# Recurrent stage of a decoder step: normalisation moved to mid-turn, a convolution ahead of the output, the store on another queue

## What is computed

```python
def rglru_block(h, conv_buf, h0, w_in, conv_w, conv_b, w_a, b_a, w_x, b_x, lam, w_out):
    gate_in, xb = jnp.split(h @ w_in, 2, axis=-1)
    gate = jax.nn.gelu(gate_in)
    xcat = jnp.concatenate([conv_buf.astype(xb.dtype), xb], axis=1)
    xc = conv_b + sum(xcat[:, j:j + T] * conv_w[j] for j in range(CONV_W))
    r = jax.nn.sigmoid(einsum('btnc,ncd->btnd', xcb, w_a) + b_a)      # xcb: xc in 8 blocks of 128
    i = jax.nn.sigmoid(einsum('btnc,ncd->btnd', xcb, w_x) + b_x)
    log_a = -RG_C * r * jax.nn.softplus(-lam)
    a = jnp.exp(log_a)
    u = jnp.sqrt(-jnp.expm1(2.0 * log_a)) * (i * xc)
    ...                                   # h_t = a_t * h_(t-1) + u_t along the tokens
    y = hs.swapaxes(0, 1).astype(h.dtype) * gate
    return y @ w_out, hT.astype(h.dtype), new_buf
```

## Time and profile before

| | |
|---|---|
| median of 3 runs | 5921.05 us |
| the profiled execution | 5920.19 us, span 5918.3 us |
| TensorE matmul busy | 4575.7 us (77%) |
| VectorE busy | 2266.9 us (38%) |
| ScalarE busy | 1815.5 us (31%) |
| recurrent stage | about 3860 to 4960 us of the span |

### The profile page before, as it was taken

The page is one execution under the profiler, slowest core; times in us unless marked ns, Lnnn a source line. Parts: engine busy times, 40 slices in busy tenths (PEclk is TensorE's granted clock), DMA queues, the critical chain, the costliest instruction groups (busy, mean ns, idle before and its releaser), DMA issues. The chain is left out here.

```text
span 5918.3 us, 54940 instructions
## 1 busy us (share of the span) xinstructions
PE 4575.7 (77%) x15227; PEld 2364.3 (40%) x15228; DVE 2266.9 (38%) x5727; ACT 1815.5 (31%) x3166; POOL 622.8 (11%) x781
## 2 busy tenths in 40 slices
PE   7999547789999987886557999268888875499970
PEld 2444212233333332333254444155666554444430
DVE  1111365566655577624332111444444332411115
ACT  0111146666666632231121222122222221122212
POOL 0111200000001100111210101200000001110113
PEclk9999657899999999897757999679888975599985
DMA  7111100000000000005256777711000002268765
GB/s 259 55 51 40 60 8 13 13 13 9 11 13 15 17 16 18 17 22 211 88 195 254 275 276 260 295 45 42 22 21 21 28 20 64 106 207 288 290 236 185
DMA packets 153251, 603.54 MB, mean 102 GB/s; under 512 B 24575, under 2 KB 27007, under 8 KB 134120
## 3 DMA queue, kind: packets, MB, share of 16 engines
q1 hardware_dynamic: 97946, 407.29, 19.5%
q0 software_dynamic: 34208, 119.30, 5.7%
q10 hardware_dynamic: 20928, 75.00, 3.1%
HBM read 466.97 MB, written 134.61 MB: 102 GB/s over the span
## 5 line engine op out<-in xcount | busy, mean ns | idle before, releaser
L2218 PE MATMUL experts_ps_gu<-w_sb,experts_xT 128*128 x1504 | 680.2, 606 | 39.1 <-DMA w_sb<-moe_w_in 34.7
L1025 PE MATMUL attend_po<-attend_PT,V 128*128 128x512 f32 x1088 | 593.0, 671 | 32.9 <-ACT attend_total L755 32.9
L2735 PE MATMUL recurrent_psAB<-recurrent_hT,rec_w_in_sb 128*128 128x256 f32 (+1 forms) x2304 | 534.7, 391 | 10.6 <-ACT recurrent_hT L2530 10.6
L469 PE MATMUL project_pj<-project_w,project_hT 128*128 128x512 f32 (+2 forms) x1360 | 506.9, 530 | 6.6 <-ACT project_proj L385 5.5
L2735 PEld LDWEIGHTS recurrent_psAB<-recurrent_hT,rec_w_in_sb 128*128 128x128 f32 x2304 | 462.7, 215 | 76.5 <-issue 11.7
L782 ACT ACTIVATE attend_passed<-attend_score,attend_cand 128x1152 bf16<-128x1152 f32 (+8 forms) x279 | 439.9, 1577 | 133.4 <-DVE attend_cand L892 110.8
L2218 PEld LDWEIGHTS experts_ps_gu<-w_sb,experts_xT 128*128 128x128 f32 x1504 | 285.2, 195 | 368.9 <-issue 368.9
L745 ACT ACTIVATE attend_PT<-attend_big 128x512 f32<-128x512 f32 x544 | 293.6, 592 | 397.8 <-PE attend_big L1014 396.8
L834 DVE CUSTOM_DVE_ANT_0 attend_junk<-attend_aux,attend_hide 128x512 bf16<-128x512 f32 (+3 forms) x640 | 364.4, 608 | 104.4 <-PE attend_aux L1034 102.1
L1034 PE MATMUL attend_aux<-attend_KTb,attend_qTb 64*128 64x512 bf16 (+3 forms) x640 | 182.5, 386 | 227.2 <-DVE attend_mx L834 198.2
L2208 PE MATMUL experts_ps_y<-w_sb,experts_midT 128*128 x752 | 342.4, 598 | 11.4 <-issue 11.4
(11 more groups left out here) (463 smaller groups left out, 5585.0 us busy)
## 6 DMA issues: line engine op xcount, KB each, us to landing
w_sb<-moe_w_in SPq DMA_DIRECT2D x64, 2048.0 KB, 11.4
w_sb<-moe_w_in SPq DMA_DIRECT2D x64, 1024.0 KB, 8.4
yb_scratch<-experts_y ACTq DMA_DIRECT2D x94, 512.0 KB, 8.7
index_slab<-ada_w_in SPq DMA_DIRECT2D x12, 2048.0 KB, 9.7
route_x<-xa_scratch SPq DMA_DIRECT2D x32, 512.0 KB, 4.7
hs_scratch<-route_h ACTq DMA_DIRECT2D x32, 512.0 KB, 4.8
yb_scratch<-route_blank SPq DMA_DIRECT2D x32, 512.0 KB
combine_x<-xa_scratch SPq DMA_DIRECT2D x32, 512.0 KB, 7.2
```

The costliest lines, as they stand in the source:

```text
L469: last = pe.matmul(pj[0:rows, bank, 0:c1 - c0], hT[:, b, k, 0:rows], w[:, k, c0:c1], start=(k == 0), stop=(k == KC - 1))
L1025: pe.matmul(po[:, n % 2, :], V1[:, b, n, :], PT[:, g % 4, :], start=(b == 0), stop=(b == S[i] // NKV - 1)).then_inc(pv_done, 1)
L2218: last = pe.matmul(ps_gu[:, u, :], xT[:, u, k, :], w1[:, bass.ds(slot, 1), k, :].rearrange("p a n -> p (a n)"), start=(k == 0), stop=(k == ...
L2735: last = pe.matmul(psAB[:, c % 2, part, 0:W], w_in[:, k, part * D + c * P:part * D + (c + 1) * P], hT[:, k, 0:W], start=(k == 0), stop=(k ...
```

## The change

Four edits, all in `phase_recurrent`:

1. ScalarE takes the squares of the next turn's tokens at c = 3, between Tanh and gates(2), instead of at c = 7.
2. VectorE's `start(q+1)` (the next turn's norm) stands behind L2673 of chunk 4 instead of behind that of chunk 7.
3. The convolution is a function `conv(q, c, W, rows)`. That of chunk 0 of the next turn is called behind the scans and ahead of the output instructions; in the body the convolutions of chunks 1 to 7 stay where they were. Ahead of the first turn and of the sample turn it is called behind `start`.
4. The stores of `out` go from ScalarE's queue to SyncE's, each behind the load of `res` of its tile and a wait for its sum; the last wait for all stores goes with them.

TensorE's and GpSimd's code is unchanged.

```diff
@@ sync
                         sy.wait_ge(res_done, t)
                         sy.dma_start(res[0:rows, :], tile_rows(src, t, rows)).then_inc(res_in, 16)
+                        sy.wait_ge(res_done, t + 1)
+                        sy.dma_start(tile_rows(dst, t, rows), out[0:rows, :]).then_inc(res_out, 16)
                 blocks(sy, body, start)
+                sy.wait_ge(res_out, 16 * (2 * NQ + 1))
                 sy.wait_ge(ends_done, 2)
@@ scalar
-                        if ahead and c == KC - 1:
+                        if ahead and c == 3:
                             squares_of(q + 1, rows)
...
                     act.activation(root[:, :, 0:W], root[:, :, 0:W], ACT.Sqrt).then_inc(sqrt_done, 1)
-                    for t, i in tiles(q, rows):
-                        act.wait_ge(res_done, t + 1)
-                        act.dma_start(tile_rows(dst, t, rows), out[0:rows, :]).then_inc(res_out, 16)
 
                 blocks(act, body, start)
-                act.wait_ge(res_out, 16 * (2 * NQ + 1))
@@ vector
+                def conv(q, c, W, rows):
+                    n = q * KC + c
+                    cat, o = xcat[:, c % 2, :], xc[:, c % 2, 0:W]
+                    dve.wait_ge(xb_copied, 2 + n + 1)
+
+                    dve.wait_ge(ri_done, n + 1)
...
+                    dve.sem_inc(conv_done, 1)
...
+                        if c:
+                            conv(q, c, W, rows)
                         dve.wait_ge(gx_squared, n + 1)
...
-                    if ahead:
-                        start(q + 1, W, rows)
+                        if ahead and c == 4:
+                            start(q + 1, W, rows)
                     weigh(KC - 1)
...
+                    if ahead:
+                        conv(q + 1, 0, W, rows)
                     for t, i in tiles(q, rows):
                         dve.wait_ge(res_in, 16 * (t + 1))
...
-                blocks(dve, body, start)
+                start(0, WB, P)
+                conv(0, 0, WB, P)
+                with dve.Fori(0, NQ - 1) as q:
+                    body(q, WB, P, True)
+                body(NQ - 1, WB, P, False)
+                start(NQ, NS, NS)
+                conv(NQ, 0, NS, NS)
+                body(NQ, NS, NS, False)
```

More of the change, by code:

```diff
@@ L2632, in start @@
                         dve.tensor_tensor(h[0:rows, i], h[0:rows, i], shift[0:rows, :], ALU.add).then_inc(x_used, 1)
+                def conv(q, c, W, rows):
[3 more added lines that the diff above has]
+                    dve.wait_ge(ri_done, n + 1)
+                    if rows == P:
+                        dve.tensor_copy(cat[:, 1:4], carry[:, :, c])
+                        dve.drain()
+                        taps = [cat[:, 1 + j:1 + j + W] for j in range(CONV_W)]
+                    else:
+                        old = state[:, c, 0:NS * (CONV_W - 1)].rearrange("p (b j) -> p j b", j=CONV_W - 1)
+                        taps = [old[:, j, :] for j in range(CONV_W - 1)] + [cat[:, 4:4 + W]]
+                    dve.tensor_scalar(o, taps[0], par[:, 0, c:c + 1], par[:, 4, c:c + 1], ALU.mult, ALU.add)
+                    if rows == P:
+                        dve.tensor_copy(carry[:, :, c], cat[:, 1 + W:4 + W])
+                    else:
+                        dve.tensor_copy(xb_s[:, c, :], cat[:, 4:4 + W])
+                    dve.drain()
+                    for j in range(1, CONV_W):
+                        dve.scalar_tensor_tensor(o, taps[j], par[:, j, c:c + 1], o, ALU.mult, ALU.add)
+                        dve.drain()
+                    dve.sem_inc(conv_done, 1)
                 def body(q, W, rows, ahead):
```

## The result

The changed kernel takes 5888.88 us (median of 5 runs, 5881.42 to 5897.94) against 5921.05 us: a ratio of 0.9942, 95% interval 0.9931 to 0.9954. It is 32 us faster; forecast were 5890.6 us, 30.5 us faster. The profiled execution is the fastest of the five, 5881.42 us with a span of 5879.4 us.

What follows compares the result with a forecast made beforehand. TensorE sets the pace, busy 99.52 of 119.40 us a turn. Per turn 6.0 + 4.95 - 5.05 - 1.36 = 4.54 us, seven times 31.8, less 1.3: 30.5 us faster, 5890.6 us; range 5863 to 5906.

Steps and rivals of the forecast that it cites:

- The gap ahead of the transposes: TensorE between recur(7) and the transposes: moving squares and norm gains 6.0 us a turn of the 7.7 us gap.
- The mid-turn cost: Ahead of project(5) and project(7): moved squares and norm exceed the ring's slack, 5.05 us lost a turn; bounds 0 and 7.4.
- the rival of hidden squares and norm (B): Mid-turn: moved squares and norm cost nothing and leave no gap; 45 us better, 5846 us; chance 0.08.
- The clock: TensorE's clock behind the 3.4 us mid-turn gap: 1.36 us lost a turn, bounds 0 and twice that.
- The gap behind the output: From the last output matmul to project(2): early convolution and moved stores gain 4.95 us a turn; project(2) left at 8.26 us.
- The jump to the loop's head: VectorE, from the sum at loop end to the polynomial at its head: 0.46 us taken, bounds 0 and 0.8.
- E: The end of the output matmuls on TensorE, 4256.03 before; project(2) was forecast about 4.4 us behind it.
- Rival C: Behind the output: the gap stays because something else holds VectorE or ScalarE; 35 us missing, 5925 us; chance 0.07.
- Rival D: Mid-turn: the clock stays down until past the second gap, projects 5 and 6 at half speed; slower, 5963 us; chance 0.05.
- Project(0) to the output: TensorE's stretch from project(0) to the output matmuls: stays 16.14 us, nothing gained; at most 1.2 us a turn with warmer clock.
- The ends: Ahead of the sample turn 0.6 us, at the stage's end 0.7 us for the last store: 1.3 us lost once.
- The sum: Whole kernel: 4.54 us gained a turn, 31.8 over seven turns, less 1.3: 30.5 us faster, 5890.6 us.

Runs made afterwards that it cites:

- the repeat: The changed kernel run once more with nothing altered, for a second profile and the spread: 5883.70 us, ratio 0.9930 to the kernel before.
- the norm edits alone: The kernel before with only the squares at c = 3 and the norm behind chunk 4, convolution and stores as before: 5922.81 us, ratio 0.9999.
- the control with `weigh` moved: The kernel before with only weigh(c-1) put behind VectorE's product of chunk c: 5923.84 us, ratio 0.9997.

## Why the prediction was right, step by step

**The gap ahead of the transposes.** Forecast: project(0) 6.0 us sooner, ScalarE's gates next. Measured: 19.26 - 13.23 = 6.03 us, and the wait is ended by ScalarE's copy (4.84 us). Right.

**The mid-turn cost.** Forecast: gaps of about 1.6 and 3.4 us, 5.05 us in all. Measured as idle 1.49 and 3.02; from start to start, recur(3) at 4042.22 to project(5) at 4044.74 is 2.52 us and recur(5) to project(7) 4.05, each for 0.87, 4.8 us in all. Right in its size and in what ends the gaps, and it is why the rival of hidden squares and norm (B) fell. That the new gaps come from the product's place behind the gates was shown by moving `weigh`: the first went whole, of the second 1.07 us stayed, and 25 us came back. The loads of `x`, now issued later, are hidden as forecast: the squares start at 4039.01 without a wait.

**The clock.** Behind the 3 us gap the forecast took 1.36 us a turn. The seven projects(7) take, from start to start, 6.98, 6.98, 9.97, 8.46, 6.98, 9.95 and 8.47 us where 6.91 is full speed: a mean of 1.35 more. The size was right, the picture was not: it isn't paid evenly but as 0, 3 and 1.5 us by turn. Windows of the changed kernel (length, busy PE PEld DVE ACT POOL, clock, DMA): behind that gap in turn 1, then the gap and the stretch behind it in turn 2.

```profile
4063.50:4066.50 3.00, 2.96 (x14) 2.65 (x15) 2.51 (x7) 0.00 (x0) 0.00 (x0) 1.00 0.00 0
4172.80:4175.80 3.00, 0.07 (x1) 0.00 (x0) 1.24 (x4) 2.21 (x6) 0.00 (x0) 0.89 0.00 0
4175.80:4178.80 3.00, 2.91 (x7) 2.38 (x8) 2.48 (x8) 0.00 (x0) 0.00 (x0) 0.50 0.00 0
```

The same gap, once followed by full clock (2.4 GHz), once by half (1.2 GHz). The warning of the Trainium skill (TensorE: Matmul & The Clock Gate, Why this matters for your kernels) against idle gaps between bursts holds behind this gap in four of seven turns here, and in five of seven in the repeat. That the mean came out at 1.35 for a forecast of 1.36 is luck: in the repeat it is 1.75.

**The gap behind the output.** This term was mis-sized twice, both times too small. The jump to the loop's head was taken at 0.46 us (0.4 in its sum); VectorE in the changed kernel:

```profile
4129.07 1.23 DVE L2711 TENSOR_TENSOR recurrent_out<-recurrent_out,recurrent_res 128x1024 f32<-128x1024 f32 x1
4130.21 0.29 DVE L2670 TENSOR_SCALAR recurrent_gx<-recurrent_gx 128x256 f32<-128x256 f32 x1
```

The sum stands at the end of the loop, the polynomial at its head, and the second starts before the first is over: the jump costs nothing. Project(2) starts 3.80 us behind E (4132.05 - 4128.25), not 4.4, so 5.5 us were gained for 4.95. And project(2) was left at 8.26 us; with a gap of 2.93 us it takes 6.98 in five turns of seven and 8.67 in two, 7.46 on average: 0.8 us a turn better. The prediction had up to 1.36 for this as a bound and nothing in the sum. Rival C, that the gap stays, fell. Rival D, the clock down until past the second mid-turn gap, fell too: projects 5 and 6 run at 6.98 and 6.91 us.

**Project(0) to the output.** Taken at 16.14; measured 15.5 to 16.9, 16.3 on average. Nothing was won there, as said. The transposes of tile 0 now stand right behind matmuls at full clock and take 1.04 us instead of 1.94, but those of tile 1 take 1.94 again, and project(0) starts at half clock, as this window shows:

```profile
4083.70:4086.70 3.00, 2.95 (x7) 2.44 (x8) 0.00 (x0) 2.99 (x2) 0.00 (x0) 0.50 0.00 0
```

By the Trainium skill's rule on transposes (TensorE: Matmul & The Clock Gate, Part 4), which the prediction weighed, this is what was to be expected. But TensorE is also idle for 4.84 and 1.30 us in this stretch, which could bring the clock down by itself, and no run here tells the two apart. The Trainium skill also says there that full clock doesn't engage for transposes; here eight of them take 1.04 us behind matmuls at full clock and 1.94 at half, so they run at the clock that is granted.

**The ends.** Forecast 1.3 us lost. Ahead of the sample turn TensorE waits 12.63 us for 11.61, 1.0 more; from the last sum to the next stage's first load (not in the lines shown) 15.7 us for 15.2, 0.5 more. About 1.5.

**The sum.** 6.0 + 5.5 - 4.8 - 1.35 + 0.8 - 0.2 = 5.95 us a turn, with the two clock terms as means over seven turns; the six periods of the two profiles give 119.4 - 113.8 = 5.6, and over those same six turns project(7) costs 1.55 and project(2) brings 0.7, which makes 5.65. The forecast had 4.54: the term of the gap behind the output was too small by 0.55, that of project(2) by 0.8. In the medians this is hidden: 32 us for a forecast of 30.5, with an interval of 27.2 to 40.9 us (0.9954 and 0.9931). The stage itself, from TensorE's first work in it to the next stage's first transposes, is 39.0 us shorter in the profile (1110.1 and 1071.1 us) and 34.4 in that of the repeat, whose medians differ by 41.3 us (33.8 to 49.2). So the mechanism of each gap held and the time lies within the stated bounds, but that it was met to 2 us is in part luck: the sum was some 4 to 9 us too small.

## What to carry to other kernels

A step moved into a stretch where an engine is busy under half of the time isn't free when that stretch is a closed ring across engines: count the ring's slack against the engine that sets the pace, once for each chunk. What is over is paid: here 7.4 us were added, 2.35 of slack were counted, and 4.8 were lost. Before a step is moved, look for what it waits behind on its own engine; here the norm needed none of the gates ahead of it, and putting it ahead of them, with `weigh` behind the product, brought, with the squares in mid-turn, 5.3 of the 6.0 us without the two gaps that the move to mid-turn cost. And test the halves of a change alone: one of these two brought nothing measurable.

## What was not expected of the hardware

An idle gap of TensorE of the same 3.02 us was followed by full clock in three turns and by half clock in four, at a cost of 1.5 or 3.0 us; over the turns it follows an order (the periods 112.3, 114.0 and 115.1 us, repeated), not chance. Nor does the length of a gap decide it: behind the same 2.11 us ahead of recur(7) the first matmul pair takes over 0.8 us, partly at half clock, in six of seven turns of the kernel before, and 0.53 to 0.54 us, at full clock, in all seven of the changed kernel. And three kernels whose gaps differ, the one before, the norm edits alone and the control with `weigh` moved, settle at the same period, 119.45 to 119.47 us: what the gaps gave there, colder matmuls took back. Why, no run here shows. The jump from a loop's end to its head cost VectorE no measurable time, where the 0.46 us on ScalarE in the earlier trace rows had looked like such a jump.
